# The delta rule of a two-block transformer kernel: the same steps, interleaved in another order

## The chip, the cores and the metric

The kernel runs on one core of a Trainium2 chip. It is one launch that computes two transformer blocks one after the other, in float32. The metric is the device time of the launch in microseconds (us). The kernel before takes 2214.82 us, the median of three runs (2214.7, 2214.82 and 2216.09).

## The reference, cut to what matters

The first block (stick-breaking, forgetting and memory attention, then an MLP) and the later parts of the second (band attention, cross-attention, gated MLP) are not touched by the change. What is touched is the second block's delta rule: 8 heads of width 128, over 512 positions in 8 chunks of 64.

```python
h = rmsnorm_2(x, norm_mix[l])
qa, ka, va, za, alpha, beta, qb, kb, vb, ga, gb = _split_cols(h @ w_in[l], IN_SPLITS)
qkv = jax.nn.silu(_causal_dwconv(jnp.concatenate([qa, ka, va], axis=-1), conv_w[l]))
qa, ka, va = _split_cols(qkv, (A_QK, A_QK, A_VW))
oa = _gated_deltanet(qa, ka, va, alpha, beta, a_log[l], dt_bias[l])
oa = rmsnorm_2(oa, head_norm[l]) * jax.nn.silu(za.reshape(b, s, A_HEADS, A_DV))
...
# in _gated_deltanet, for every head and chunk
q = _l2norm(...) * (A_DK ** -0.5); k = _l2norm(...)
kk = jnp.einsum("bhncd,bhnjd->bhncj", k, k)
L = jnp.where(strict, beta[..., :, None] * kk * decay, 0.0)
sol = lax.linalg.triangular_solve(jnp.eye(CHUNK, dtype=f32) + L, rhs, left_side=True,
                                  lower=True, unit_diagonal=True)
...
def step(S, inp):
    ut, wt, pt, qt, kt, et = inp
    U = ut - jnp.einsum("bhck,bhkv->bhcv", wt, S)
    o = jnp.einsum("bhck,bhkv->bhcv", qt, S) + jnp.einsum("bhcj,bhjv->bhcv", pt, U)
    S = S * et[..., None, None] + jnp.einsum("bhck,bhcv->bhkv", kt, U)
    return S, o
```

For each head there are thus four weight products (columns of q, k, v and z), a convolution, silu and l2 norm of what they give, a preparation that needs no state (the triangular solve), and a scan over 8 chunks that does, with a norm and a gate behind it.

## The kernel before, in words

All weights are float32 and come from one packed tensor, in_wall, by DMA into tiles called stage. ScalarE (ACT) rounds a stage tile to its high part whi (L1785), and VectorE (DVE, L2255) or GpSimd (POOL, L2843) subtracts it to get the low part wlo. In the delta rule POOL does this. A block of a weight product is three matmuls of TensorE (PE) with 512 columns: hh with whi (L1258), hl with whi (L1260), hh with wlo (L1264). A product step, called mm, is two blocks, six matmuls; an output tile of 128 columns takes four such steps.

Every small piece of work is a step with a name. The steps of a stretch lie in strands, each with a fixed order of its own, and a string of letters says from which strand the next step is taken. `Schedule.paced` does this:

```python
order = ORDERS[key]
left = [iter([s for s in c if s[0][0] not in ("need", "mark")]) for c in strands]
for c in order:
    yield next(left[ord(c) - 97])
```

The one sequence that comes out is then walked once for each of the five engines (PE, ACT, DVE, POOL, and SP, which issues DMAs), so a string sets the order on all five queues. No engine reorders anything; a wait at the head of a queue holds all that stands behind it. Semaphores carry the dependences, and a buffer that is written again waits until its last reader is done.

The delta rule has nine intervals. The opening (string gdn) has as strand a the products of head 0, as b the scalars of all heads (`gdn_scalars`), as c the convolutions, silu and l2 norm of head 0 (`gdn_proj`). Then comes head h for h from 0 to 8 (strings head0, head1, head for h = 2 to 5, head6, head7, head8). In interval h, strand a is the 16 products of head h+1, b its convolutions, silu and l2 norms (with the gate of head h), c the scan of head h-1 (`gdn_scan`), and d the preparation of head h (`gdn_prep`); in head0 there is no scan, so c is the preparation. In head7 and head8 the products are those of the following gates.

The steps that matter below:

- gs_rows: two small results of 8 x 512 (the decays by row), copied out by ACT (L2076, L2078), stored to DRAM (rows, rowsc) and read back spread over all partitions (gbc). decay(0) on POOL and ACT (L2084) needs them, and gp_xy(0) on PE needs that.
- gp_kk, gp_xy, gp_P(n) and gp_Y(n) for n = 1 to 5, gp_uw: the triangular solve by repeated squaring. gp_P(n) writes bank 3 with 8 matmuls of 64 x 64; DVE copies it to an ya tile; gp_Y(n) reads that. gp_uw is the application to both right sides (8 matmuls from 64 x 128, 8 to 128 x 64). gp_kk of the next head reads nothing of it but writes bank 4, which gp_uw fills and ACT empties (L2110).
- gc_w(n), gc_s(n): the scan of chunk n. gc_w is cs with cwt and cqd with cs; DVE takes the difference (cuu); gc_s is cuu with ckd and cpt with cuu; DVE updates cs.
- The head norm behind gc_s(7): gc_o (ACT L2115, copy), hn_sq (ACT L1859) and oq (POOL, cu<-cu,gq), hn_split (ACT L1864 to oah, DVE to oal), hn_mm (PE: two matmuls of 512 columns from oah and oal), hn_out and the gate. The l2 norms have the same hn_mm.

A row of PE names the output and the moving operand as out<-in; 64*64 beside it is the part of the array that is used.

Of the kernel before, what the change touches and what calls it, by code (L numbers as in the profile page):

```python
# [30 lines left out]
for _n, _w in VECS:  # L31
# [19 lines left out]
    "fox1": "fagafgaafgaafgfbaafbagfbgfaaggcagfacfagfgcafdaafgadgadafgfe",  # L51
    "fox2": "fgfagaagagfgaffggabfaabbagfagfgagcafgacffgagcgagafgdagfadfgdagagef",
    "fox3": "bacacabcacbaaacbbccaabbcacaacabcacaaccbaacbabacbaacbacbcacacb",
    "gdn": "aaaaaccbcaaacabacccccacbcaaaaacccacccabaac",
    "head0": "caacaaacbcababbabcaacabbbbcbbabaacaabcbbaccbbacababc",
    "head1": "acdcacdaaabcdbcdbbbaacdacacdcababbcbbdacdcdcbbabacabdcbacbdaccbacdabcadbc",
    "head": "acdcadcaacddabbcbbbaaacdcdacadcabbbbcdabcacbbdcabcadbbcabcbdaccadcabcadbc",
    "head6": "dcacdacdacaabbaacbbdbcadacdacbbabcbdbacbbacdbcdcdabcabdcacbaccbadabcacdbc",
    "head7": "dcdacdacacacdcaacdcacacacadacbdacdcdcdacdccadacdcc",
    "head8": "abababaababababaababababaababababaabbaabababab",  # L60
    "band": "caaccacaacacacacaacacbcacacacac",
    "band3": "caacacaacbcacaacaccaaccacacacac",
    "band4": "caacaacaccacaacbcaaaacacacaacacaaacc",
# [3059 lines left out]
```

How the kernel before makes its waits and increments, by code:

```python
    def free(use):  # L1215
        for ref in use.before:
            if fresh(*ref):
                pe.wait_ge(*at(*ref))
# [1 line left out]
    def wait(*refs):  # L1220
        for ref in refs:
            if fresh(*ref):
                pe.wait_ge(*at(*ref))
# [19 lines left out]
    def product(g, x):  # L1243
        o = bank[g.use.bank][:, 0:g.n]
        if x == 0:
            free(g.use)
        for j in (x, x + 1):
            unit, n = divmod(g.blocks[j], UNIT)
            c = slice(128 * n, 128 * n + 128)
            wh, wl = k.whi[unit % NSPLIT][:, c], k.wlo[unit % NSPLIT][:, c]
            hi, lo, hi_refs, lo_refs = moving(g, g.ks[j])
            if "c0" in g.a:
                half = slice(g.a["c0"], g.a["c0"] + g.n)
                hi, lo = hi[:, half], lo[:, half]
            if fresh("whi", unit):
                pe.wait_ge(*at("whi", unit))
            wait(*hi_refs)
            pe.matmul(o, wh, hi, start=j == 0, stop=False)
            wait(*lo_refs)
            pe.matmul(o, wh, lo, start=False, stop=False)
            if fresh(k.lo_sem[unit], unit):
                pe.wait_ge(*at(k.lo_sem[unit], unit))
            end = j == len(g.ks) - 1
            i = pe.matmul(o, wl, hi, start=False, stop=end)
            if end or n == UNIT - 1:
                i.then_inc(*up("pe_w", *([("unit", unit)] if n == UNIT - 1 else []), *([g.key] if end else [])))
# [21 lines left out]
    def seven(p, i):  # L1288
# [2 lines left out]
            free(use)  # L1291
        elif i == 2:
            pe.wait_ge(*at("sv_p0", p.no))
        elif i == 4:
```

## Time and profile before

| | |
|---|---|
| time, median of three runs | 2214.82 us (2214.7 to 2216.09) |
| span of the profiled execution | 2214.8 us |
| PE busy | 2194.2 us, 99% |
| weight load of PE busy (PEld) | 1806.3 us, 82% |
| DVE busy | 1279.5 us, 58% |
| ACT busy | 1010.5 us, 46% |
| POOL busy | 442.4 us, 20% |
| DMA | 199.69 MB, mean 90 GB/s |

The profiled execution has the span alone as its time. Matmuls overlap and their ends are modelled, so the busy time of PE hides short waits. The start of a weight load (engine PEld in the trace) shows when PE goes on to a new matmul: the distance from one start to the next is what a step costs, and the bracket behind a row shows how long the load unit stood idle before it and on what. "issue" there is idle time with no releaser in the profile. A row with xN joins N like instructions that follow each other.

The delta rule runs from 900.3 us (its first product) to about 1270 us, where interval 8 begins.

### The profile page before, as it was taken

Reading aid. Unit: us, or ns where it says so; the run is one execution under the profiler, and the core shown is the slowest. Engines: PE = TensorE matmul, PEld = TensorE weight load, DVE = VectorE, ACT = ScalarE, POOL = GpSimd, SP = SyncE. Lnnn points to the kernel's source line nnn. Section 1 sums busy time; section 2 is a strip of 40 time slices with the busy share of each in tenths; the row PEclk is TensorE's granted clock in tenths of the full one; section 3 lists DMA queues with packets and bytes.
Section 4 is the critical chain, followed back from the end, with each engine's and each line's share of the span. In section 5 each row is a group of like instructions: output and inputs, shape, how many; then the busy total and the mean of one; then the engine's idle time right before and its main releaser. Section 6 shows DMA issues by size and latency. Waiting matters only on the chain.

```text
span 2214.8 us, 35833 instructions
## 1 busy us (share of the span) xinstructions
PE 2194.2 (99%) x13488; PEld 1806.3 (82%) x13488; DVE 1279.5 (58%) x2431; ACT 1010.5 (46%) x1902; POOL 442.4 (20%) x364
## 2 busy tenths in 40 slices
PE   9999999999999999999999999999999999999998
PEld 7777778888888888778888887777788888889887
DVE  5545755445744646576666524665556557757464
ACT  6555654334533534445545333444535545434244
POOL 2443220001201102433533451000011001101001
PEclk9999999999999999999999999999999999999999
DMA  5223222333323333321121134233233513323333
GB/s 184 77 69 104 72 58 80 93 99 96 97 94 105 100 100 96 94 89 54 57 79 45 39 92 128 77 88 85 67 96 110 142 54 95 106 86 115 96 96 95
DMA packets 108650, 199.69 MB, mean 90 GB/s; under 512 B 12208, under 2 KB 14384, under 8 KB 108224
## 3 DMA queue, kind: packets, MB, share of 16 engines
q1 hardware_dynamic: 108480, 197.41, 30.0%
q8 instruction: 108, 1.77, 0.3%
q14 instruction: 62, 0.51, 0.1%
HBM read 195.20 MB, written 2.16 MB: 89 GB/s over the span
## 4 chain that ended last, share of the span: by engine, by line
PE 95%; DVE 2%; ACT 1%; DMA 1%; issue 1%; SPq 0%; POOL 0%; DVEq 0%; ACTq 0%; POOLq 0%
PE bank L1258 24%; PE bank L1264 23%; PE bank L1260 23%; PE bank L1210 20%; PE bank L1213 3%; PE bank L1279 1%; PE bank L1284 0%; PE bank L1282 0%; SPq L2954 0%; DMA x<-in_xT 0%; DMA stage<-in_wall 0%; DVE gq L2258 0%; DVE fout L2255 0%; DVE acc L2255 0%; ACT sbA L1967 0%
## 5 line engine op out<-in xcount | busy, mean ns | idle before, releaser
L1785 ACT ACTIVATE whi<-stage 128x512 fp32r<-128x512 f32 x668 | 414.9, 626 | 472.5 <-PE bank L1264 415.6
L1258 PE MATMUL bank<-hh,whi 128*128 128x512 f32 x1456 | 590.1, 405 | 0.3 <-ACT bv L1876 0.3
L1264 PE MATMUL bank<-hh,wlo 128*128 128x512 f32 x1456 | 569.8, 391 | 0.6 <-DVE wlo L2255 0.6
L1260 PE MATMUL bank<-hl,whi 128*128 128x512 f32 x1456 | 568.4, 390 | 0.0
L2255 DVE TENSOR_TENSOR wlo<-stage,whi 128x512 fp32r<-128x512 f32 x492 | 378.9, 787 | 62.5 <-ACT whi L1785 58.1
L1264 PEld LDWEIGHTS bank<-hh,wlo 128*128 128x128 f32 x1456 | 273.6, 188 | 61.3 <-DVE wlo L2255 2.1
L1258 PEld LDWEIGHTS bank<-hh,whi 128*128 128x128 f32 x1456 | 273.9, 188 | 56.6 <-issue 1.6
L1260 PEld LDWEIGHTS bank<-hl,whi 128*128 128x128 f32 x1456 | 274.2, 188 | 53.1 <-issue 1.2
L2843 POOL TENSOR_TENSOR wlo<-stage,whi 128x512 fp32r<-128x512 f32 x176 | 238.8, 1365 | 359.8 <-ACT whi L1785 359.7
L2255 DVE TENSOR_TENSOR x<-bank,x 128x512 f32<-128x512 f32 (+1 forms) x81 | 55.5, 685 | 170.3 <-PE bank L1264 170.2
L2843 POOL TENSOR_TENSOR acc<-acc,sqb 128x512 f32<-128x512 f32 x34 | 45.7, 1345 | 278.5 <-ACT sqb L1798 278.5
L1258 PE MATMUL bank<-u1h,whi 128*128 128x512 f32 x256 | 99.6, 389 | 0.0
L1260 PE MATMUL bank<-u1l,whi 128*128 128x512 f32 x256 | 99.6, 389 | 0.0
L1264 PE MATMUL bank<-u1h,wlo 128*128 128x512 f32 x256 | 99.6, 389 | 0.0
L2843 POOL TENSOR_TENSOR u1l<-f1t,u1h 128x512 fp32r<-128x512 f32 x32 | 43.9, 1371 | 257.1 <-ACT u1h L1940 179.0
L1210 PE MATMUL bank<-ya 64*64 64x64 f32 (+2 forms) x2048 | 72.0, 231 | 0.8 <-DVE ya L2255 0.7
L1210 PEld LDWEIGHTS bank<-ya 64*64 64x64 f32 (+1 forms) x2048 | 58.5, 137 | 17.3 <-issue 11.7
L1258 PE MATMUL bank<-u2h,whi 128*128 128x512 f32 (+1 forms) x182 | 69.7, 383 | 0.0
L1260 PE MATMUL bank<-u2l,whi 128*128 128x512 f32 (+1 forms) x182 | 69.6, 383 | 0.0
L1264 PE MATMUL bank<-u2h,wlo 128*128 128x512 f32 (+1 forms) x182 | 69.5, 382 | 0.0
L1210 PE MATMUL bank<-th,whi 128*128 128x256 f32 x224 | 63.4, 283 | 0.0
L1210 PE MATMUL bank<-tl,whi 128*128 128x256 f32 x224 | 63.4, 283 | 0.0
(440 smaller groups left out, 4014.8 us busy)
## 6 DMA issues: line engine op xcount, KB each, us to landing
stage<-in_wall SPq DMA_DIRECT2D x682, 256.0 KB, 2.7
band<-in_toep SPq DMA_DIRECT2D x16, 256.0 KB, 3.4
x<-in_xT SPq DMA_DIRECT2D x8, 256.0 KB, 5.7
fb<-rowsf SPq DMA_DIRECT2D x8, 256.0 KB, 3.7
gbc<-rows SPq DMA_DIRECT2D x8, 256.0 KB, 3.2
gbc<-rowsc SPq DMA_DIRECT2D x16, 128.0 KB, 3.6
out_y<-fout SPq DMA_DIRECT2D x8, 256.0 KB, 2.6
memx<-in_memT SPq DMA_DIRECT2D x1, 1024.0 KB, 9.5
```

The lines of the kernel that those rows point to most:

```text
L1210: return pe.matmul(out, w, r, start=start, stop=stop, skip_group_check=True)
L1213: return pe.transpose(out, in_, k.cf("ident"))
L1258: pe.matmul(o, wh, hi, start=j == 0, stop=False)
L1260: pe.matmul(o, wh, lo, start=False, stop=False)
L1264: i = pe.matmul(o, wl, hi, start=False, stop=end)
L1279: pe.matmul(o, hi[:, tokens], wh, start=x == 0, stop=False)
L1785: act.activation(k.whi[u % NSPLIT][:], k.source(u), ACT.Copy).then_inc(*up("whi", u))
L2255: return dve.tensor_tensor(out, a, b, op)
L2843: return pool.tensor_tensor(out, a, b, op)
```

## The change

Seven strings of `ORDERS` are replaced: gdn, head0, head1, head, head6, head7, head8. Each new string holds each letter as often as the old one, so each strand keeps its own order and no step is added, removed or altered; only where the strands are cut into each other differs. The string head is used four times. Two of the seven lines:

```diff
-    "gdn": "aaaaaccbcaaacabacccccacbcaaaaacccacccabaac",
+    "gdn": "aaaaaacccbcaaaaacacbacaacacccababcccaacccca",
...
-    "head": "acdcadcaacddabbcbbbaaacdcdacadcabbbbcdabcacbbdcabcadbbcabcbdaccadcabcadbc",
+    "head": "aacdcacdadcadbbacbaacabdcdaabcbdbbacbdbacacdcabbacdbcabdbbcaccbdcaabbcdcc",
```

On PE, the end of interval 3 (string head, the same in intervals 2 to 5): cpt0,cuu01 is gc_s(7) of the scan of head 2, bank3<-ya 64x64 is gp_P(5), bank4<-ya 64x64 is gp_Y(5), oah and oal are hn_mm, bank3<-ya 64x128 is the begin of gp_uw. A step of products is six rows; only its first rows are shown. Before:

```order
L1210 MATMUL bank6<-cpt0,cuu01 128x64
L1258 MATMUL bank1<-hh,whi0 128x512
...
L1210 MATMUL bank3<-ya 64x64 x8
L1258 MATMUL bank1<-hh,whi0 128x512
...
L1258 MATMUL bank1<-hh,whi1 128x512
...
L1210 MATMUL bank4<-ya 64x64 x8
L1210 MATMUL bank6<-oah,onr2 128x512
L1210 MATMUL bank6<-oal,onr2 128x512
L1258 MATMUL bank1<-hh,whi1 128x512
...
L1210 MATMUL bank3<-ya 64x128 x8
```

And now:

```order
L1210 MATMUL bank3<-ya 64x64 x8
L1210 MATMUL bank6<-cpt0,cuu01 128x64
L1258 MATMUL bank1<-hh,whi1 128x512
...
L1210 MATMUL bank4<-ya 64x64 x8
L1258 MATMUL bank1<-hh,whi1 128x512
...
L1210 MATMUL bank6<-oah,onr2 128x512
L1210 MATMUL bank6<-oal,onr2 128x512
L1210 MATMUL bank3<-ya 64x128 x8
```

Between the last scan step and the head norm stood three product steps, gp_P(5) and gp_Y(5); now two product steps and gp_Y(5) stand there, and the head norm has moved right ahead of gp_uw.

On PE, the seam from interval 5 to interval 6 (string head6): ya 64x128 and ya 128x64 are gp_uw of head 5, gk 64x64 is gp_kk of head 6, cu,ckd and cpt,cu are the first scan step of head 5. Before:

```order
L1210 MATMUL bank<-ya 64x128 x8
L1210 MATMUL bank<-ya 128x64 x8
L1210 MATMUL bank<-gk 64x64 x8
L1210 MATMUL bank<-cu,ckd 128x128
L1210 MATMUL bank<-cpt,cu 128x64
L1258 MATMUL bank<-hh,whi 128x512
```

And now:

```order
L1210 MATMUL bank<-ya 64x128 x8
L1210 MATMUL bank<-ya 128x64 x8
L1258 MATMUL bank<-hh,whi 128x512
L1260 MATMUL bank<-hl,whi 128x512
L1264 MATMUL bank<-hh,wlo 128x512
L1258 MATMUL bank<-hh,whi 128x512
L1260 MATMUL bank<-hl,whi 128x512
L1264 MATMUL bank<-hh,wlo 128x512
L1210 MATMUL bank<-cu,ckd 128x128
L1210 MATMUL bank<-cpt,cu 128x64
L1210 MATMUL bank<-gk 64x64 x8
```

A product step and the scan step now stand between gp_uw and gp_kk, which followed each other before.

On ACT, the opening (string gdn): ya<-bank 8x512 are the copies of gs_rows, sqb and oah the l2 norm of k of head 0. Before:

```order
L2094 ACTIVATE gk<-gk 128x512
L2094 ACTIVATE gq<-gq 128x512
L1775 ACT_TABLE_LOAD
L1785 ACTIVATE whi<-stage 128x512
L1859 ACTIVATE sqb<-gk 128x512
L2076 ACTIVATE ya<-bank 8x512
L2078 ACTIVATE ya<-bank 8x512
L1864 ACTIVATE oah<-sqb 128x512
L1785 ACTIVATE whi<-stage 128x512 x2
L1825 ACTIVATE sqb<-bank,eps 128x512
```

And now:

```order
L1785 ACTIVATE whi<-stage 128x512
L2094 ACT_TABLE_LOAD
L2094 ACTIVATE gk<-gk 128x512
L2094 ACTIVATE gq<-gq 128x512
L1775 ACT_TABLE_LOAD
L1859 ACTIVATE sqb<-gk 128x512
L1864 ACTIVATE oah<-sqb 128x512
L1785 ACTIVATE whi<-stage 128x512
L2076 ACTIVATE ya<-bank 8x512
L2078 ACTIVATE ya<-bank 8x512
L1825 ACTIVATE sqb<-bank,eps 128x512
```

The copies of the decay rows have moved behind the split of the l2 norm and one more rounding of weights.

## Rows read from the trace of the kernel before

**Rows 1.** The page: busy times, and the chain that ended last.

```profile
PE 2194.2 (99%) x13488; PEld 1806.3 (82%) x13488; DVE 1279.5 (58%) x2431; ACT 1010.5 (46%) x1902; POOL 442.4 (20%) x364
...
PE 95%; DVE 2%; ACT 1%; DMA 1%; issue 1%; SPq 0%; POOL 0%; DVEq 0%; ACTq 0%; POOLq 0%
```

**Rows 2.** Timeline of PE's weight loads: start, us, engine, line, output<-input, [idle before].

```profile
1089.69 0.19 PEld L1258 LDWEIGHTS bank<-hh,whi 128*128 128x128 f32 x1
...
1091.29 0.54 PEld L1210 LDWEIGHTS bank<-ya 64*64 64x64 f32 x16 [0.36 <-issue]
1091.90 0.19 PEld L1258 LDWEIGHTS bank<-hh,whi 128*128 128x128 f32 x1
...
1093.16 0.19 PEld L1258 LDWEIGHTS bank<-hh,whi 128*128 128x128 f32 x1
...
1094.84 0.54 PEld L1210 LDWEIGHTS bank<-ya 64*64 64x64 f32 x16 [0.35 <-issue]
```

**Rows 3.** The same view, the second half of gp_uw at the ends of intervals.

```profile
1055.90 0.97 PEld L1210 LDWEIGHTS bank<-ya 64*128 64x128 f32 x16 [0.17 <-issue]
1098.52 0.97 PEld L1210 LDWEIGHTS bank<-ya 64*128 64x128 f32 x16 [0.17 <-issue]
1183.77 0.97 PEld L1210 LDWEIGHTS bank<-ya 64*128 64x128 f32 x16 [0.17 <-issue]
1229.52 0.97 PEld L1210 LDWEIGHTS bank<-ya 64*128 64x128 f32 x16 [0.17 <-issue]
1267.40 0.97 PEld L1210 LDWEIGHTS bank<-ya 64*128 64x128 f32 x16 [0.17 <-issue]
```

**Rows 4.** Timeline of the opening and head 0: POOL, and PE's loads.

```profile
936.40 0.63 POOL L2843 TENSOR_TENSOR ya<-gbc,gcolS 128x256 f32<-128x256 f32 x1 [4.68 <-DMA gbc<-rowsc]
...
938.79 0.13 PEld L1210 LDWEIGHTS bank<-cft,ya 64*64 64x64 f32 x1 [1.45 <-DVE ya L2255]
...
963.55 0.56 PEld L1210 LDWEIGHTS bank<-ya 64*64 64x64 f32 x32 [0.37 <-issue]
964.77 0.54 PEld L1210 LDWEIGHTS bank<-ya 64*64 64x64 f32 x16 [0.67 <-DVE ya L2255]
```

**Rows 5.** Timeline of ACT at the decay rows.

```profile
927.49 0.57 ACT L2078 ACTIVATE ya<-bank 8x512 f32<-8x512 f32 x1
927.97 0.61 ACT L1864 ACTIVATE oah<-sqb 128x512 fp32r<-128x512 f32 x1
928.49 1.14 ACT L1785 ACTIVATE whi<-stage 128x512 fp32r<-128x512 f32 x2
```

**Rows 6.** Timeline of all engines, head norm in interval 1.

```profile
1004.23 0.30 PEld L1210 LDWEIGHTS bank<-cpt,cuu 128*128 128x128 f32 x2
...
1007.48 0.63 ACT L1864 ACTIVATE oah<-cu 128x512 fp32r<-128x512 f32 x1 [1.45 <-POOL cu L2843]
1008.14 1.10 DVE L2255 TENSOR_TENSOR oal<-cu,oah 128x512 fp32r<-128x512 f32 x1 [0.88 <-ACT oah L1864]
```

**Rows 7.** The same in interval 3.

```profile
1089.47 0.30 PEld L1210 LDWEIGHTS bank<-cpt,cuu 128*128 128x128 f32 x2
...
1094.82 1.07 POOL L2843 TENSOR_TENSOR ya<-gbc,gcolS 128x256 f32<-128x256 f32 x1
...
1095.45 0.19 PEld L1210 LDWEIGHTS bank<-oah,onr 128*128 128x128 f32 x1
1095.56 0.19 PEld L1210 LDWEIGHTS bank<-oal,onr 128*128 128x128 f32 x1
```

**Rows 8.** The same in interval 7.

```profile
1260.07 0.30 PEld L1210 LDWEIGHTS bank<-cpt,cuu 128*128 128x128 f32 x2
...
1264.04 0.68 DVE L2255 TENSOR_TENSOR oal<-cu,oah 128x512 fp32r<-128x512 f32 x1
```

**Rows 9.** Timeline of PE's loads, intervals 6 and 7.

```profile
1185.76 0.58 PEld L1210 LDWEIGHTS bank<-gk 128*64 128x64 f32 x16 [1.02 <-issue]
...
1215.84 0.19 PEld L1210 LDWEIGHTS bank<-oal,onr 128*128 128x128 f32 x1 [0.54 <-DVE oal L2255]
...
1231.51 0.58 PEld L1210 LDWEIGHTS bank<-gk 128*64 128x64 f32 x16 [1.02 <-DVE ya L2258]
```

**Rows 10.** Windows: width, busy (x) of PE, PEld, DVE, ACT, POOL; PEclk, DMA share, GB/s.

```profile
937.00:940.00 3.00, 1.97 (x39) 1.35 (x38) 0.85 (x2) 1.46 (x3) 2.84 (x5) 1.00 0.38 103
...
1187.20:1190.60 3.40, 3.40 (x18) 2.69 (x21) 0.32 (x2) 0.42 (x1) 3.32 (x5) 0.51 0.23 38
```

**Rows 11.** Timeline of PE's loads: gp_uw of head 3, then a product.

```profile
1097.50 0.85 PEld L1210 LDWEIGHTS bank<-ya 64*64 64x64 f32 x16 [0.35 <-issue]
...
1099.56 0.19 PEld L1258 LDWEIGHTS bank<-hh,whi 128*128 128x128 f32 x1
```

More of the change, by code:

```diff
@@ L53 @@
     "fox3": "bacacabcacbaaacbbccaabbcacaacabcacaaccbaacbabacbaacbacbcacacb",
-    "gdn": "aaaaaccbcaaacabacccccacbcaaaaacccacccabaac",
-    "head0": "caacaaacbcababbabcaacabbbbcbbabaacaabcbbaccbbacababc",
-    "head1": "acdcacdaaabcdbcdbbbaacdacacdcababbcbbdacdcdcbbabacabdcbacbdaccbacdabcadbc",
-    "head": "acdcadcaacddabbcbbbaaacdcdacadcabbbbcdabcacbbdcabcadbbcabcbdaccadcabcadbc",
-    "head6": "dcacdacdacaabbaacbbdbcadacdacbbabcbdbacbbacdbcdcdabcabdcacbaccbadabcacdbc",
-    "head7": "dcdacdacacacdcaacdcacacacadacbdacdcdcdacdccadacdcc",
-    "head8": "abababaababababaababababaababababaabbaabababab",
+    "gdn": "aaaaaacccbcaaaacacbacaacacccababcccaacccca",
+    "head0": "caaacaaaccbbbaabacabacbbabbbbcbaacaaabcabcaccabbbbbc",
+    "head1": "acdcacdacdaacbbdbabbacdacacdcaacbbbbacabdcbdabcdbacdcccabbaadcabdbccbdacb",
+    "head": "aacdcacdadcadbbacbaacabdcdaabcbdbbacbdbacacdcabbacdbcabdbbcaccbdcaabbcdcc",
+    "head6": "acdcacdadcaababcacbdbabcdacadbabcbabbcbdcdbacdbcdabcdcabcacabcdabaacdbcbc",
+    "head7": "acbdcaccdcadadcaacdcdaacaacacdcdacdcacdcadccdcadcc",
+    "head8": "abababaabababababaababababaabababaabbabaabbaab",
     "band": "caaccacaacacacacaacacbcacacacac",
```

## The prediction

> **What bounds the kernel now.** I read the page first: PE is busy for 99% of the span and makes 95% of the chain that ended last, while DVE stands at 58%, ACT at 46% and POOL at 20% [rows 1]. So the time is the sum of what PE's steps cost, plus the short waits that stand between them. The busy time does not show these, because the ends of matmuls are modelled; the starts of the weight loads do. I therefore read the loads next, and after them the engines that PE waits for. The change alters no step, so it can act in only three ways: on what a step costs behind another kind of step, on the waits, and on the granted clock.
>
> The price of a step is the distance of two starts [rows 2]. A product step behind a small step takes 1.26 us (1091.90 to 1093.16). The next one takes 1.68 (1093.16 to 1094.84), and the load unit is idle for 0.35 before the 64*64 group that follows. Without that I price a product behind a product at 1.37, six matmuls at about 0.23, so the turn to a group of 64 rows costs 0.31. A group of 64*64 matmuls takes 0.61 (1091.29 to 1091.90).
>
> An interval is the distance of one gp_uw to the next [rows 3]: 42.62 for interval 3 (1098.52 less 1055.90), 85.25 for intervals 4 and 5 together, so again 42.62 each. Interval 6 takes 45.75 and interval 7 takes 37.88. Intervals 6 and 3 hold about the same work, so interval 6 loses about 3.1 us, and that is what the change could win.
>
> **The opening and head 0 (strings gdn and head0): plus 1.35.** In the trace gp_xy(0) waits until 938.79, with the load unit idle for 1.45 [rows 4]; less the turn to 64 rows that is a wait of 1.1. It hangs on the decay rows: the second ACT copy begins at 927.49 [rows 5], the rows come back for POOL at 936.40 [rows 4]. In the changed order the copies stand behind the split of k's l2 norm and one more rounding. On PE gs_rows now stands 5.4 us of products later. Laid end to end with the ACT durations of [rows 5], the copies begin about 2.1 us later, since ACT and not PE held them before. gp_xy(0) could then start at 940.9. PE arrives with one product more in between, at 937.7 plus 1.37, so at 939.05: a wait of 1.85 in place of 1.1, plus 0.75. The bounds: if the copies are not later, the wait of 1.1 vanishes (minus 1.1); if they are later by the full 5.4, it is plus 4.0. I take 0.75, as ACT's own queue is the nearest thing to a row here.
>
> At the end of head 0, gp_P(5), gp_Y(5) and gp_uw now follow each other with nothing between. The nearest row is gp_P(5) behind gp_Y(4): it starts 1.22 after it (963.55 to 964.77), where 0.61 would do without a wait [rows 4]. That wait of 0.6 goes, since a product stands there now, and two of 0.65 to 0.75 come, because each group needs DVE's copy of the one before: plus 0.8 (between 0, if DVE answers within the group, and 1.4). Head 0 has a few turns less, minus 0.2. Sum 1.35.
>
> **Interval 1 (head1): 0.** Turns and waits come out level within 0.2; bounds minus 0.7 (all its waits) and plus 1.
>
> **Intervals 2 to 5 (head, used four times): plus 1.3 each, 5.2 in all.** This is the main term. The products are cut into 15 runs instead of 12. Each cut makes one product cheaper by 0.11 and adds a turn of up to 0.31 where a 64-row group follows; by the sequence of steps that is plus 0.5.
>
> The head norm is the other part. Its chain starts with gc_s(7) and runs over ACT, ACT with POOL, ACT and DVE. In interval 1 gc_s(7) starts at 1004.23; the high half oah is ready at 1008.11 (1007.48 and 0.63), 3.9 later, and the low half oal at 1009.24 (1008.14 and 1.10), 5.0 later [rows 6]. In interval 3 hn_mm stands 5.98 behind gc_s(7) on PE [rows 7], so the chain is covered. In the new order there stand between them: gc_s(7) 0.2, a product with a turn 1.6, gp_Y(5) 0.61, a product 1.26, which is 3.7. The first matmul then waits 0.2 and the second until 5.0, so PE stands for 1.1. Directly behind it is gp_uw of the same interval, on which the whole next interval hangs, so nothing wins it back. Below, in interval 7, DVE made the same split in 0.68 and the low half was there 4.65 behind gc_s(7) [rows 8], which leaves a wait of 0.75. Above, gc_o waits on ACT behind a rounding and an activation of about 0.6 each, which makes it 2.0.
>
> What speaks for the higher price is that DVE and POOL slow each other. POOL's subtraction of 128x256 takes 0.63 with DVE idle [rows 4], and 1.07 beside the split [rows 7]; the split takes 1.10 there and 0.68 with POOL idle [rows 6, 8]. The Trainium skill has this as a rule (GPSIMD Engine Reference, the key points: GpSimd shares its SBUF interfaces with VectorE, and contends with VectorE instructions that have two SBUF inputs). By that rule the split, which reads two SBUF tiles, is slow only where POOL runs; then the wait is 1.1 where POOL has a low half to make and 0.75 where not, and the sum would be 4.4 or 3.0. The trace agrees, 1.10 against 0.68.
>
> Minus 0.3 comes from gp_uw to the next scan: two products instead of one stand behind it, so the small waits of gc_s(0) and its like go. So 0.5 plus 1.1 less 0.3, 1.3 per interval; between 0.2 (no wait for the norm) and 2.2 (a wait of 2.0).
>
> **Interval 6 (head6): minus 2.55.** Three things go. First, gp_kk(6) follows gp_uw(5) directly and writes the bank that ACT still empties. From the second half of gp_uw to the next start it takes 1.99 [rows 3, 9] against 1.04 where a product follows (1098.52 to 1099.56) [rows 3, 11]; 0.95 goes, as a product and a scan step stand between now. Second, the granted clock fell to 0.51 for 3.4 us right after that gap [rows 10], the lower of its two levels; half of 3.4 is 1.7 lost, less a wait that was there anyway, 1.5. Third, the l2 norm of k waits 0.54 for its low half [rows 9], 0.6 with what is ahead of it; two products cover it now. With 0.3 of small waits 3.35 goes. Against that stand 0.3 for turns and 0.5 for small waits between scan steps that follow closer. Minus 2.55; between minus 3.4 and minus 1 (where the clock falls all the same).
>
> **Intervals 7 and 8 (head7, head8): plus 0.4.** The same wait of gp_kk behind gp_uw goes (0.95 and 0.3 more) [rows 9]. What comes: gp_Y(5) directly behind gp_P(5), 0.65; gc_s(1) and gc_w(2) adjacent, 0.35; the head norm 0.15 and small waits 0.5. That is 1.65 less 1.25. Between minus 1.2 and plus 1.2. String head8 moves a few scan steps among products, 0.
>
> **The sum.** 1.35 plus 0 plus 5.2 less 2.55 plus 0.4 is plus 4.4, on a span of 2214.8, which is also the median of the runs (2214.82). So 2219.2. What a measurement of this kernel can tell from no change is about 0.2%, 4.4 us: the forecast is slower, and lies on that border.
>
> One more rule bears on the turns. What the rows show is 0.35 of idle load time before a 64*64 group behind a product, and none before the product behind it [rows 2]. The Trainium skill (TensorEngine Tiling (Array Packing), Tiling Modes) says that changing the tiling mode drains TensorE, without a direction. By the rows the turns of the whole stretch (36 before a 64-row group, now 41) make 1.5, and that is in the sum; by the rule both directions would pay, and it would be 3.1.
>
> **The rivals.**
> - The head norm's wait is not an added one (not slower). While PE waits for oal, DVE finishes gp_Y(5)'s copy and the l2 and convolution work, so that gp_uw and the first steps of the next interval start without their small waits; and where POOL is idle the wait is 0.75. It decides where what is saved behind comes near 1.1 per interval. For it: 0.17 before the second half of gp_uw [rows 3], and the many idle gaps of a few tenths. Against it: those come to some 0.3 per interval. Price: four times minus 1.0, so 4.4 less 4.0, 2215.2.
> - The clock falls again. It fell after a gap of 1.02, but not after 1.45 in head 0 (1.00 from 937 to 940) [rows 9, 10], nor at 1231.51. The new order has at least six gaps of 0.6 to 1.9. One to three falls at 1.5: 2220.7 to 2223.7.
> - Only the gains are real (faster): the rows come back in time (minus 1.1 instead of 0.75), and the head norm's wait and turns come to nothing. 4.4 less 1.85 less 4.8 is minus 2.2, 2212.6. Against it: the chain of 4.65 at best is longer than 3.7.
> - Both directions of a turn pay: 1.5 more, 2220.8. Against it: no idle time before the product rows.
>
> **How the numbers follow.** The forecast has 0.45, the norm without price 0.25, the clock 0.17, only the gains 0.08, the drain in both directions 0.05. The forecast is split at the border, half of it same and half slower. Slower: 0.22, 0.17 and 0.05, about 0.45. Faster: about half of the case with gains alone passes 4.4, and some of the others, where more than I see is won; I give 0.08. The rest, 0.47, is the same. The range reaches from 2213.5, between the two low cases, to 2223, inside the upper end of the clock's case; the forecast's own range is 2217 to 2221.5.
>
> **What would show it.** In the profile after: in intervals 2 to 5 a load of oal,onr with about 1 us idle before it, on DVE oal, and gp_uw to gp_uw about 43.9 in place of 42.6; without that the main term is wrong. The load of cft,ya of head 0 idle for about 2.2 on DVE ya. No 1.02 before the gk load of heads 6 and 7, a clock of 1.00 there, and interval 6 at about 43.2, interval 7 at about 38.3. What would make it wrong: a lower clock in any repeated interval, or ACT queueing gc_o later than in interval 1.

## The result and the profile after

The changed kernel takes 2220.97 us (median of 7 runs, 2220.38 to 2222.7), the kernel before 2215.03 us beside it (7 runs, 2214.19 to 2216.09). That is 5.9 us or 0.27% slower: the ratio is 1.0027, with a 95% interval of 1.0016 to 1.0038. The forecast was 2219.2.

The page of the changed kernel, the rows that answer to [rows 1]:

```profile
PE 2193.4 (99%) x13488; PEld 1804.1 (81%) x13488; DVE 1281.7 (58%) x2431; ACT 1010.6 (46%) x1902; POOL 435.9 (20%) x364
...
PE 94%; DVE 2%; ACT 2%; DMA 1%; issue 1%; SPq 0%; POOL 0%; DVEq 0%; ACTq 0%; POOLq 0%
```

Nothing on the page has moved by more than a point; PE's busy time has even fallen. The loss is in the starts. These are the ends of the intervals, gp_uw's second half, answering to [rows 3]:

```profile
969.68 0.97 PEld L1210 LDWEIGHTS bank<-ya 64*128 64x128 f32 x16 [0.17 <-issue]
1012.37 0.97 PEld L1210 LDWEIGHTS bank<-ya 64*128 64x128 f32 x16 [0.17 <-issue]
1057.30 0.97 PEld L1210 LDWEIGHTS bank<-ya 64*128 64x128 f32 x16 [0.17 <-issue]
1101.55 0.97 PEld L1210 LDWEIGHTS bank<-ya 64*128 64x128 f32 x16 [0.17 <-issue]
1145.82 0.97 PEld L1210 LDWEIGHTS bank<-ya 64*128 64x128 f32 x16 [0.17 <-issue]
1190.07 0.97 PEld L1210 LDWEIGHTS bank<-ya 64*128 64x128 f32 x16 [0.17 <-issue]
1233.73 0.97 PEld L1210 LDWEIGHTS bank<-ya 64*128 64x128 f32 x16 [0.17 <-issue]
1271.42 0.97 PEld L1210 LDWEIGHTS bank<-ya 64*128 64x128 f32 x16 [0.17 <-issue]
```

Their distances, beside those of before from the same rows of its trace (us):

| interval | string | before | after | difference |
|---|---|---|---|---|
| first product to the end of 0 | gdn, head0 | 69.91 | 70.41 | +0.5 |
| 1 | head1 | 43.08 | 42.69 | -0.4 |
| 2 | head | 42.63 | 44.93 | +2.3 |
| 3 | head | 42.62 | 44.25 | +1.6 |
| 4 | head | 42.61 | 44.27 | +1.7 |
| 5 | head | 42.64 | 44.25 | +1.6 |
| 6 | head6 | 45.75 | 43.66 | -2.1 |
| 7 | head7 | 37.88 | 37.69 | -0.2 |
| 8 and all behind it | head8 | 947.4 | 947.7 | +0.4 |

The sum is plus 5.4. The last row of the table is no result: over all fourteen profiles of this document the stretch from there to the end takes 946.8 to 947.8, with either string head8. The spans, 2219.2 and 2214.8, differ by 4.4 only: the changed kernel reached the first product of the stretch 1.0 earlier. In the profiled execution of before the granted clock had fallen for 3.4 us at 101.8, in a part that no changed string touches:

```profile
101.00:106.00 5.00, 4.32 (x17) 2.19 (x18) 0.91 (x2) 2.00 (x5) 1.26 (x1) 0.66 0.18 52
```

and in that of the changed kernel it had not (the columns as in [rows 10]):

```profile
101.00:106.00 5.00, 3.71 (x27) 2.31 (x28) 1.36 (x3) 2.58 (x7) 1.27 (x1) 1.00 0.19 54
```

Eight of the fourteen profiles have that fall, whatever their strings, and reach the first product at 899.9 to 901.4; the six without it reach it at 898.2 to 899.3.

What PE's loads waited for from 900 to 1347 us in the changed kernel (sum, times, longest):

```profile
PEld bank L1210 <- DVE ya L2255: 8.6, 12, 1.5
PEld bank L1210 <- DVE oal L2255: 4.1, 4, 1.0
PEld bank L1210 <- ACT oah L1864: 1.3, 4, 0.3
```

In the same view of before stood 3.2 us for ya and 0.5 for oal:

```profile
PEld bank L1210 <- DVE ya L2255: 3.2, 6, 1.5
...
PEld bank L1210 <- DVE oal L2255: 0.5, 1, 0.5
```

Both new waits come once in each of the four intervals of the string head. In interval 3, PE's loads first:

```profile
1067.45 0.57 PEld L1210 LDWEIGHTS bank<-ya 64*64 64x64 f32 x16 [0.67 <-DVE ya L2255]
...
1094.92 0.30 PEld L1210 LDWEIGHTS bank<-cpt,cuu 128*128 128x128 f32 x2
...
1098.88 0.19 PEld L1210 LDWEIGHTS bank<-oah,onr 128*128 128x128 f32 x1 [0.32 <-ACT oah L1864]
1100.10 0.19 PEld L1210 LDWEIGHTS bank<-oal,onr 128*128 128x128 f32 x1 [1.03 <-DVE oal L2255]
```

The last two are the head norm that was forecast. gc_s(7) starts at 1094.92 and oal can be loaded at 1100.10, 5.2 later; the forecast had 5.0. The first row is gp_P(1), which was not forecast. The rows of DVE and POOL in front of each tell why it waits:

```profile
1066.15 1.19 DVE L2255 TENSOR_TENSOR ya<-cft,ya 128x256 f32<-128x256 f32 x1
...
1098.86 1.18 DVE L2255 TENSOR_TENSOR oal<-cu,oah 128x512 fp32r<-128x512 f32 x1 [0.98 <-ACT oah L1864]
```

```profile
1065.76 1.29 POOL L2843 TENSOR_TENSOR wlo<-stage,whi 128x512 fp32r<-128x512 f32 x1
...
1098.12 0.63 POOL L2843 TENSOR_TENSOR ya<-gbc,gcolS 128x256 f32<-128x256 f32 x1
1098.83 0.67 POOL L2843 TENSOR_TENSOR ya<-ya,cbt 128x256 f32<-128x256 f32 x1
```

A DVE operation of 128x256 that otherwise takes 0.43 takes 1.19, because POOL had begun a low half 0.39 us earlier; it ends 0.29 after POOL does (1067.34 against 1067.05). The Trainium skill (SBUF — State Buffer, SBUF: two separate sides) says that the port pair of VectorE and GpSimd is an exclusive lock, which whoever starts first holds for its whole instruction. That is what these rows look like, and all rows of the stretch bear it out. In the changed kernel from 900 to 1271 us, ten operations ya<-cft,ya of 128x256 began at least 0.15 ahead of the end of one of POOL: they took 0.52 to 1.56, and each ended 0.28 after POOL's did. Nine splits of 128x512 to oal did, and each ended 0.55 after it, the 1.18 above among them (POOL's ends at 1099.50). Where POOL began second, the same DVE operations took 0.43 and 0.68 to 0.69, as they do alone. The twenty ya<-bank,cft that began beside POOL, with one input from a bank, took 0.41 to 0.43 all the same. So the delay depends on when POOL began; the prediction had priced it as a fixed slowing.

### The profile page after: what moved, and what is told of

It is laid out like the page before. It is cut to its first block, busy times and chain, and to the rows that moved or that the text cites. A ratio compares the mean times of both kernels' runs of the same rounds, so it can differ in the third digit from the quotient of the medians.

```text
span 2219.2 us, 35830 instructions
## 1 busy us (share of the span) xinstructions
PE 2193.4 (99%) x13488; PEld 1804.1 (81%) x13488; DVE 1281.7 (58%) x2431; ACT 1010.6 (46%) x1902; POOL 435.9 (20%) x364
## 3 DMA queue, kind: packets, MB, share of 16 engines
q8 instruction: 108, 1.77, 0.3%
## 4 chain that ended last, share of the span: by engine, by line
PE 94%; DVE 2%; ACT 2%; DMA 1%; issue 1%; SPq 0%; POOL 0%; DVEq 0%; ACTq 0%; POOLq 0%
PE bank L1258 23%; PE bank L1264 23%; PE bank L1260 23%; PE bank L1210 20%; PE bank L1213 3%; PE bank L1279 1%; PE bank L1282 0%; PE bank L1284 0%; DVE ya L2255 0%; DMA x<-in_xT 0%; DMA stage<-in_wall 0%; SPq L2954 0%; POOL cu L2843 0%; DVE fout L2255 0%; DVE acc L2255 0%
## 5 line engine op out<-in xcount | busy, mean ns | idle before, releaser
L1260 PE MATMUL bank<-u2l,whi 128*128 128x512 f32 (+1 forms) x182 | 69.6, 383 | 0.0
```

The source lines that it names most:

```text
L1260: pe.matmul(o, wh, lo, start=False, stop=False)
```

## The experiments

Differences are medians against before, measured again in the same series, or against the changed kernel's 2220.97 of the first series. The medians of before go from 2214.19 to 2215.33 over the series, so a difference to the changed kernel is known to about 1 us only. Single executions of one kernel spread by up to 4.8 us. The mechanism is therefore read from the intervals of the profile, which repeat to about 0.05 us where the clock is 1.00 and the strings ahead are the same (one exception: interval 2 took 43.03 and 42.65 in the two tries at the end).

**The string head alone.**

```diff
# before
-    "head": "acdcadcaacddabbcbbbaaacdcdacadcabbbbcdabcacbbdcabcadbbcabcbdaccadcabcadbc",
+    "head": "aacdcacdadcadbbacbaacabdcdaabcbdbbacbdbacacdcabbacdbcabdbbcaccbdcaabbcdcc",
```

> The kernel before with the new string head alone (intervals 2 to 5). My theory: the whole loss of the change sits in these four intervals, from gp_uw to gp_uw 44.3 us instead of 42.6 (the head norm's low half waited for about 1 us, gp_P(1) behind gp_xy about 0.7), so 6.5 to 7.5 us slower than before, more than the whole change. Rival (cost of turns to 64-row groups spread over the stretch): four intervals at 0.5, 2 us slower.

Measured 2220.58 against 2214.66 (33 runs), ratio 1.0024 (1.0016 to 1.0033): plus 5.9, as much as the whole change, a little under the range. Intervals 2 to 5 took 43.9, 44.3, 44.3 and 44.3. The rival of spread turns is out. The seam into interval 6 is the old one here, and this profile gave what the prediction needed and did not have, the price of that seam without a fall of the clock:

```profile
1190.53 0.58 PEld L1210 LDWEIGHTS bank<-gk 128*64 128x64 f32 x16 [1.02 <-DVE ya L2258]
```

```profile
1190.50:1194.00 3.50, 3.44 (x46) 3.01 (x50) 0.91 (x3) 1.67 (x3) 2.76 (x3) 1.00 0.00 0
```

The gap of 1.02 is there, the clock stays at 1.00, and interval 6 takes 44.25 in place of 45.75. In the run of the opening alone, further below, where both head and head6 are the old strings, it takes 44.42 at a clock of 1.00, a small wait of 0.23 included. So one fall costs 1.3 to 1.5, and it does not come in every execution.

**All but the string head.** Its edit is the change without that line.

> The changed kernel with the old string head. My theory: 1 to 2.5 us faster than before (interval 6 about 43.7 instead of 45.8, interval 1 0.4 shorter, opening and head 0 0.5 longer). Rival (the clock fell in interval 6 of before by chance, not because of its gap): no difference within 0.7 us.

Measured 2213.79 against 2214.66, ratio 0.9994 (0.9985 to 1.0003): 0.9 faster by the medians, which can't be told from none. The profile has interval 1 at 42.67, interval 6 at 43.16, interval 7 at 37.68, no fall of the clock in them. Against 44.25 or 44.42 the gain of interval 6 is 1.1 to 1.3 where the clock stays.

**The head norm one place later.**

```diff
# changed kernel
-    "head": "aacdcacdadcadbbacbaacabdcdaabcbdbbacbdbacacdcabbacdbcabdbbcaccbdcaabbcdcc",
+    "head": "aacdcacdadcadbbacbaacabdcdaabcbdbbacbdbacacdcabbacdbcabdbbcaccbdcaabbdccc",
```

> The changed kernel with hn_mm of the head norm moved one place back in the string head, behind gp_uw. My theory: the wait for oal (1.03 idle) goes in intervals 2 to 5, since gp_uw's 2.06 us now lie in between: 1.1 each, 4 to 4.6 us faster than the changed kernel, at about plus 1.5 on before. Rival (the wait only covers for another one: gp_uw waits for DVE's copy of gp_Y(5) in its place): under 1.5 us faster.

Measured 2215.26 against 2214.66, ratio to before 1.0001 (0.9992 to 1.001): 5.7 faster than the changed kernel, or 5.3 where each is taken against before in its own series, more than expected. This one place accounts for nearly all of the loss. The loads at the end of interval 3:

```profile
1097.18 0.85 PEld L1210 LDWEIGHTS bank<-ya 64*64 64x64 f32 x16 [0.36 <-issue]
1098.20 0.97 PEld L1210 LDWEIGHTS bank<-ya 64*128 64x128 f32 x16 [0.17 <-issue]
1099.24 0.19 PEld L1210 LDWEIGHTS bank<-oah,onr 128*128 128x128 f32 x1
1099.35 0.19 PEld L1210 LDWEIGHTS bank<-oal,onr 128*128 128x128 f32 x1
```

No wait before oah or oal, and none has taken its place at gp_uw. Intervals 3 to 5 fell from 44.26 to 42.8, by 1.5, where the norm alone was priced at 1.1. The rest is the other wait: the row at gp_P(1) now reads

```profile
1065.70 0.57 PEld L1210 LDWEIGHTS bank<-ya 64*64 64x64 f32 x16 [0.37 <-DVE ya L2255]
```

and 0.37 is no more than the turn to 64 rows that stands there without any wait [rows 2]. The next interval starts at another offset to POOL, and the same DVE operation took 0.88 instead of 1.19; it too ends 0.28 after POOL's.

**One scan step more between gp_xy and gp_P(1).**

```diff
# changed kernel
-    "head": "aacdcacdadcadbbacbaacabdcdaabcbdbbacbdbacacdcabbacdbcabdbbcaccbdcaabbcdcc",
+    "head": "aacdcacdacdadbbacbaacabdcdaabcbdbbacbdbacacdcabbacdbcabdbbcaccbdcaabbcdcc",
```

> The changed kernel with gc_w(2) moved ahead of gp_P(1) in the string head, so that one small scan step more lies between gp_xy and gp_P(1). Theory (a fixed latency from gp_xy over two DVE operations, one of them slowed by POOL): the wait of 0.67 before gp_P(1) falls to 0.2 or 0.3, but gc_w itself has to be done, so 0.3 to 0.45 less in each of intervals 2 to 5, 1.2 to 1.8 us faster than the changed kernel. Rival (DVE is the bound there, the scan's cuu goes ahead of the copy and delays it): no gain.

Measured 2220.25 against 2214.81, ratio 1.0021 (1.0012 to 1.0031): 0.7 faster than the changed kernel, which the medians can't tell, and less than expected. The intervals can: 3 to 5 took 43.77, 0.49 less, and no wait is left at gp_P(1); the 1.19 of DVE is still there, now covered. Interval 2 took 45.14 and gave nothing, so the gain is three times 0.5.

**Both edits.**

> The changed kernel with both edits: hn_mm behind gp_uw and gc_w(2) ahead of gp_P(1). Theory: the gains do not overlap fully, since e3_norm already showed 0.37 left before gp_P(1); intervals 3 to 5 at 42.5 instead of 42.8, so 0.8 to 1.2 us below e3_norm, about 2214.2. Rival: as e3_norm.

Measured 2215.38 against 2214.81, ratio 1.0001 (0.9992 to 1.001). Intervals 3 to 5 at 42.62 against 42.79: 0.2 each, less than expected, and nothing in the time.

**Less work for GpSimd, in the kernel before and in the changed one.** Both leave out 480 of the 512 columns of each low half in the delta rule.

```diff
-            tt(k.wlo[u % NSPLIT][:], k.source(u), k.whi[u % NSPLIT][:].bitcast(F32), ALU.subtract).then_inc(*up("wlo_pool", u))
+            c = slice(0, 32 if u in k.light else 512)
+            tt(k.wlo[u % NSPLIT][:, c], k.source(u)[:, c], k.whi[u % NSPLIT][:, c].bitcast(F32), ALU.subtract).then_inc(*up("wlo_pool", u))
```

> The kernel before, with GpSimd making only 32 of the 512 columns of each low half in the delta rule (the rest of a low half is stale: the low product is left out in effect). Theory (DVE's operations with two SBUF inputs are slowed beside GpSimd): here almost all of that is covered, since only 0.3 per interval was waited, so 0 to 2 us faster. Rival (GpSimd's own queue is what everything waits for): as much faster as e8_light_after.

> The same cut of GpSimd's low halves in the changed kernel. Theory: the split of the head norm takes 0.68 instead of 1.10 and the DVE operation ahead of gp_P(1) 0.43 instead of 1.19; the wait for oal falls from 1.03 to about 0.6 and the one before gp_P(1) goes, so 1.0 to 1.2 per interval, 4 to 5 us faster than the changed kernel. Rival (plain latency, no contention): under 1 us faster.

In the kernel before: 2213.57 against 2214.81, ratio 0.9994 (0.9984 to 1.0003). Its intervals 2 to 5 took 42.59 to 42.64, as with the full work, and interval 6 took 45.72: POOL costs nothing there. In the changed kernel: 2217.67, ratio to before 1.0014 (1.0004 to 1.0023), 3.3 faster than with the full work, under the range of 4 to 5. DVE in interval 3 of it, and one row of POOL:

```profile
1065.74 0.42 DVE L2255 TENSOR_TENSOR ya<-cft,ya 128x256 f32<-128x256 f32 x1
...
1098.08 0.67 POOL L2843 TENSOR_TENSOR ya<-ya,cbt 128x256 f32<-128x256 f32 x1
1098.12 1.18 DVE L2255 TENSOR_TENSOR oal<-cu,oah 128x512 fp32r<-128x512 f32 x1 [0.98 <-ACT oah L1864]
```

The operation ahead of gp_P(1) is back at 0.42, and the wait there is gone: it was POOL, in every interval. The split of the head norm is as slow as ever and PE's 1.03 stayed, which the expectation had wrong. What holds it is not a low half but POOL's work on the next head's decay, which was left at full size: the split starts 0.04 after the POOL row shown and ends 0.55 after it. Intervals 3 to 5 fell by 0.36 each (44.26 to 43.90), interval 2 by 1.03 (44.93 to 43.90), and interval 6 by 1.04 (43.66 to 42.62), where of the idle times of 0.83 and 0.69 that it has with the full work only a turn of 0.36 is left. These add up to 3.15; the gain measured is 3.3, or 3.1 with each kernel against before in its own series.

**A product step in the seam of interval 6.** The edit also puts the scan step ahead of gp_kk, as the change does.

```diff
# before
-    "head6": "dcacdacdacaabbaacbbdbcadacdacbbabcbdbacbbacdbcdcdabcabdcacbaccbadabcacdbc",
+    "head6": "acdcdacdacaabbaacbbdbcadacdacbbabcbdbacbbacdbcdcdabcabdcacbaccbadabcacdbc",
```

> The kernel before with one product step put ahead of gc_s(0) and gp_kk at the start of string head6 (seam from interval 5 to 6), nothing else changed. Theory (the gap of 1.0 behind gp_uw is a wait for ACT to empty bank 4, and the fall of the clock follows from it): the 1.02 ahead of the gk load goes, interval 6 takes about 43.3 where the clock stays, and there is no fall of the clock in it; 1 to 2.5 us faster than before. Rival (the fall has nothing to do with the gap): only 0.95 faster in a run without a fall, and falls of 3.4 us in interval 6 remain.

Measured 2214.65 against 2215.33, ratio 0.9995 (0.9986 to 1.0005): less than expected, and not told from none. The 1.02 ahead of the gk load is gone and interval 6 took 43.54, 0.7 less than 44.25 and 0.9 less than 44.42; the clock did not fall in it. Over all profiles, it fell in interval 6 in two of the four with the old seam (before and the light one of before, not e1_head and not e10_open) and in none of the ten with a product in it. That points to the gap, but one profile each is too few to call it shown.

**The opening and head 0 alone.** The lines gdn and head0 of the change.

> The kernel before with the new strings gdn and head0 alone. My prediction gave them plus 1.35; the trace of the changed kernel says plus 0.1 at gp_xy(0) (idle 1.53 in place of 1.45, one product more already done) and plus 0.4 at the end of head 0 (idle 0.73 and 0.66 before gp_Y(5) and gp_uw, in place of 0.67). Theory: 0.5 slower than before up to gp_uw(0). Rival (the prediction's sum): 1.35.

Measured 2215.88 against 2215.33, ratio 1.0003 (0.9994 to 1.0012). From the 4400th matmul, which stands 36 us ahead of the stretch, to the second half of gp_uw(0) it took 106.29, before 105.73 and the changed kernel 106.23: plus 0.5 to 0.6, not 1.35. Counted from the first product of the stretch, the seven profiles with these two strings take 70.3 to 70.5, the five with both old ones 69.6 to 70.1.

**Only the strings that gained.** head1, head6 and head7 of the change in the kernel before.

> The kernel before with the new strings head1, head6 and head7 alone. My theory: the gains without the losses, 0.4 plus 2.1 plus 0.2, so 2 to 3 us faster than before. Rival (clock by chance): within 1 us of before.

Measured 2212.2 against 2214.66, ratio 0.9989 (0.998 to 0.9998): 2.5 faster, a version that beats both.

**Two tries to go further.** The first has head1 and head6 of the change, with my own moves in head0, head6 and head7 (the line of head1 is left out below); the second takes head7 from the change again.

```diff
# before
-    "head0": "caacaaacbcababbabcaacabbbbcbbabaacaabcbbaccbbacababc",
+    "head0": "caaacaaacbacbbbabcaacabbbbcbbabaacaabcbbaccbbacababc",
-    "head6": "dcacdacdacaabbaacbbdbcadacdacbbabcbdbacbbacdbcdcdabcabdcacbaccbadabcacdbc",
+    "head6": "acdcacdacdaabacacbbdbabcdacadbabcbabbcbdcdbacdbcdabcdcabcacabcdabaacdbcbc",
-    "head7": "dcdacdacacacdcaacdcacacacadacbdacdcdcdacdccadacdcc",
+    "head7": "acdcadcacdacdcaacdcacacacadacbdacdcdcdacdccadacdcc",
```

> A try at a better order than both: head1 of the changed kernel, head6 of it with gc_w(2) ahead of gp_P(1) and one convolution step behind gc_w(3), head7 of before with its seam like that of head6, and head0 of before with one more product ahead of gp_xy(0). Theory: e5_best less 0.7 in interval 6, 0.8 in interval 7 and 1.1 in head 0, so 4 to 5 us faster than before. Rival (the waits only move on to the next step): as e5_best, 2.5 us faster.

> e11_best2 with the string head7 of the changed kernel, since my own head7 put the four DVE operations of gp_xy(7) ahead of the update of cs and made gc_w(2) wait 1.50. Theory: interval 7 at 37.7 instead of 38.5, 0.8 below e11_best2, about 2211.4, so 3.5 to 4 us faster than before. Rival (the gain is eaten elsewhere): no difference from e11_best2.

The first: 2212.26 against 2215.33, ratio 0.9988 (0.9979 to 0.9997), 3.1 faster where 4 to 5 was expected. Head 0 gained 0.9, but interval 6 gained nothing and interval 7 lost 0.65 to before. DVE and PE's loads at the start of its interval 7:

```profile
1231.39 0.83 DVE L2255 TENSOR_TENSOR ya<-cft,ya 128x256 f32<-128x256 f32 x1
1232.15 0.41 DVE L2255 TENSOR_TENSOR ya<-bank,cft 128x256 f32<-128x256 f32 x1
1232.59 1.05 DVE L2255 TENSOR_TENSOR ya<-cft,ya 128x256 f32<-128x256 f32 x1
1233.57 0.33 DVE L2258 SCALAR_TENSOR_TENSOR cs<-cs,ceg,bank 128x128 f32<-128x128 f32 x1
```

```profile
1233.96 0.19 PEld L1210 LDWEIGHTS bank<-cs,cwt 128*128 128x128 f32 x1 [1.50 <-DVE cs L2258]
```

I had put gp_xy ahead of gc_s(1). Its four DVE operations, two of them stretched by POOL, stood ahead of the update of cs, and the scan waited 1.50. The second try: 2211.74 against 2214.19, ratio 0.9987 (0.9978 to 0.9996), 2.5 faster where 3.5 to 4 was expected, with interval 7 at 37.69 and all intervals without a fall. By the intervals it is 0.9 below the three strings of the change alone, in head 0, and level with them elsewhere (294.01 against 294.11 from gp_uw(0) to gp_uw(7)); the times of the three kernels can't be told from each other.

## Why the prediction was right, and where it was not

The sign and the range held: 2220.97 lies within 2213.5 to 2223, and the loss of 5.9 is one and a third of the 4.4 forecast. The main term is where it was put. Against the measured intervals its terms were off by plus 2.0 (intervals 2 to 5) and plus 0.45 (interval 6), and by minus 0.85 (opening and head 0), 0.4 (interval 1) and 0.6 (interval 7). That the sum came close is in part luck, since these nearly cancel.

- *The head norm, 1.1 per interval.* Right, by the mechanism and the size: oal 5.2 behind gc_s(7), and with hn_mm moved behind gp_uw no wait is left. Nothing behind it made the wait up, so the rival that had it turn costless, at 0.25, is out. The prediction had left open whether the split takes 1.10 or 0.68 there; it took 1.18, because POOL's operation on the decay began just ahead of it.
- *The rest of intervals 2 to 5.* Mis-sized: 5.2 forecast, 7.2 measured. The step that failed was the count of what stands between two dependent steps. I took the waits other than the norm's as covered, with "minus 0.3" for the small ones. Between gp_xy and gp_P(1) stood two products and two scan steps, and now one product. The chain in between is two DVE operations, 0.42 and 0.43 when they run alone, and I had not laid it out. With POOL's low half across it, one takes 1.19 for 0.43; by the light run that makes 0.36 in each of intervals 3 to 5 and 1.03 in interval 2. The light run of the changed kernel shows the cause, and the light run of before shows that there it had been covered. 1.1, 0.36 and the 0.2 of turns less small waits (0.5 less 0.3 in the prediction, not measured apart) make 1.66, the 1.6 measured in intervals 3 to 5.
- *Interval 6, minus 2.55.* Measured minus 2.1, but 1.3 to 1.5 of it is the fall of the clock in the one profiled execution of before; against 44.25 or 44.42 without a fall the gain is 0.6 to 0.8. I took an event of one execution for a property of the kernel. Of the 0.95 for the seam 0.7 to 0.9 came, and new waits ate most of the rest: 0.83 before gp_P(1), of which a turn is 0.35, and 0.69 before gc_w, where DVE had the scan's update late. They too come from POOL: with its light work only the turn is left of them and the interval takes 42.62, 1.04 less.
- *The opening and head 0, plus 1.35.* Measured plus 0.5. The copies of the decay rows did come 2.1 later: they end at 929.17 in the changed kernel, 930.2 on the scale of before, against 928.06. But the rows came back for POOL only 1.4 later, and PE had one product more behind it, 1.37, so gp_xy(0) cost no more than 0.1, and the load of cft,ya was idle for 1.53 where the prediction's sign had 2.2. The term took ACT's delay as that of the whole round trip; from the end of the copies to POOL's row it took 8.34 before and 7.66 in the changed kernel. The end of head 0 was as forecast, two waits of 0.73 and 0.66 in place of 0.67.
- *Interval 1 at 0, interval 7 at plus 0.4.* Measured minus 0.4 and minus 0.2, the same within 0.05 in every profile with these strings. Interval 8 was priced at 0, and nothing here shows otherwise.
- *The base.* I set the span of the profile, 2214.8, equal to the median of the runs. The time of an execution is 1.8 us more than its span here (medians of 1.77 to 1.82 over the series), so the profiled execution was one of about 2216.6 by this estimate, at the upper end of its kernel, with falls of the clock at 101.8 and in interval 6. That is why spans differ by 4.4 and times by 5.9. That my 2219.2 equals the span of the profile after is an accident of two errors.
- *The clock.* The rival that the clock falls in the new gaps, at 0.17, did not come: it is 1.00 in every interval of the changed kernel, for all its gaps of 1.53, 1.04 and 1.03.
- *Both directions of a turn.* Not needed: two waits and 0.2 make up intervals 3 to 5. No run tested it by itself.
- *Only the gains.* Out by its sign. Its price was also wrong in itself: the norm's 1.1 and 0.5 of turns make 6.4 in four intervals and not 4.8, so it should have stood at about 2211.0.

## What to carry to other kernels

Where a written order interleaves dependent steps, lay out the chain between each pair of them with all engines in it, and price an operation on VectorE that has two SBUF inputs at what it takes when GpSimd has just begun one, which is GpSimd's whole operation and a fixed rest: 1.19 for 0.43 was the difference between a covered and an open wait. A step that only sends work on, like a norm's last product, belongs behind the next long step, not in front of it; here one letter moved by one place was worth 5.3 to 5.7 of 5.9 us. And before a gain is built on a row of one profile, ask whether every execution has it: set the span against the times of the runs, and look at the granted clock there.

## What was not expected of the hardware

- One fall of the granted clock, 3.4 us at 1.2 instead of 2.4 GHz, cost 1.3 to 1.5 us of an interval. It followed a gap of 1.02 us at PE in two profiles of four but not the gaps of 1.0 to 1.5 elsewhere in the delta rule, before and after. What decides it stays open.
- A DVE operation with two SBUF inputs began 0.39 us after a GpSimd one of 1.29 and ended 0.29 after its end: 1.19 us for 0.43. In interval 2 it began 0.01 after one (1021.21 to 1022.50) and took 1.56, so it again ended 0.28 behind it:

```profile
1021.22 1.56 DVE L2255 TENSOR_TENSOR ya<-cft,ya 128x256 f32<-128x256 f32 x1
```

- Two SBUF inputs were not needed for that. The copy ceg<-ya of 128x8, with one input and both sides in SBUF, took 0.16 alone and 0.68 to 0.90 in four places of the changed kernel where POOL had begun first. The 86 DVE operations of the stretch that read a bank and began while POOL ran took 0.69 at most, which is what 128x512 takes alone.
